# The first weight tile on ACT's own DMA queue, and a new order of the first ACT and DVE steps, in a two-block transformer forward pass

## What is computed

```python
def rmsnorm(x, g):
    x32 = x.astype(jnp.float32)
    y = x32 * lax.rsqrt(jnp.mean(x32 * x32, axis=-1, keepdims=True) + EPS)
    return y.astype(x.dtype) * g

def dilated_mixer(h, w_in, w_out):
    ...
    proj = h @ w_in
    ...
    return y @ w_out

def first_block(x, norm_pre, norm_post, dil_w_in, dil_w_out, ...):
    h = x
    for i in range(DEPTH):
        u = rmsnorm(h, norm_pre[i])
        ...
            y = dilated_mixer(u, dil_w_in[j], dil_w_out[j])
        ...
            y = diff_mixer(u, diff_w_in[j], ...)
        h = h + rmsnorm(y, norm_post[i])
    return h

def reference(...):
    x = first_block(...)
    return second_block(x, ...)
```

## Time and profile before

| | |
|---|---|
| median of 3 runs | 2640.03 us (2639.12 to 2641.21) |
| profiled execution | 2639.08 us |
| its span on the core | 2637.8 us |
| PE busy | 2607.4 us, 99% of the span |
| DVE, POOL, ACT busy | 1250.3, 1149.4, 1038.0 us |
| share of PE in the chain that ended last | 94% |
| DMA | 282.22 MB, mean 107 GB/s |

### The profile page before, as it was taken

One profiled execution on the slowest core, in us unless ns is written; L12 is line 12 of the kernel. 1 busy time (PEld: TensorE's weight loads), 2 busy tenths in 40 slices (PEclk: granted clock), 3 DMA queues, 4 the chain that ended last, 5 costly groups with the idle time before them and its releaser, 6 DMA issues.

```text
span 2637.8 us, 35473 instructions
## 1 busy us (share of the span) xinstructions
PE 2607.4 (99%) x13561; PEld 2120.3 (80%) x13561; DVE 1250.3 (47%) x2448; ACT 1038.0 (39%) x1939; POOL 1149.4 (44%) x890
## 2 busy tenths in 40 slices
PE   8999999999999999999999999999999999999998
PEld 6888878778778877777888888887777788888887
DVE  4535354553566365446155333365544624542426
ACT  4343434443546344453333424234445233342422
POOL 4434334435343354334464445454333346444443
PEclk9999999999999999999999999999999999999999
DMA  6434343333331333234442333333222435233331
GB/s 196 131 102 121 103 113 113 112 114 103 97 105 64 103 96 88 82 95 131 138 153 86 109 96 96 96 98 117 80 81 78 150 110 175 80 112 96 96 96 64
DMA packets 215121, 282.22 MB, mean 107 GB/s; under 512 B 22016, under 2 KB 155620, under 8 KB 214184
## 3 DMA queue, kind: packets, MB, share of 16 engines
q1 hardware_dynamic: 214952, 279.95, 34.5%
HBM read 246.28 MB, written 16.84 MB: 100 GB/s over the span
## 4 chain that ended last, share of the span: by engine, by line
PE 94%; DVE 3%; ACT 1%; POOL 1%; issue 1%; DMA 0%; ACTq 0%; DVEq 0%; POOLq 0%
PE banks L1808 37%; PE banks L1805 30%; PE banks L1801 13%; PE banks L1826 2%; PE banks L1940 1%; PE banks L1865 1%; PE banks L1922 1%; PE banks L2043 1%; PE banks L2070 1%; PE banks L1974 1%; PE banks L1908 1%; PE banks L2028 1%; PE banks L2056 1%; DVE AR L2553 1%; PE banks L1996 1%
## 5 line engine op out<-in xcount | busy, mean ns | idle before, releaser
L3179 POOL TENSOR_TENSOR WS<-WR,WS 128x512 fp32r<-128x512 f32 (+2 forms) x672 | 857.6, 1309 | 1015.8 <-ACT WS L2188 1015.8
L1808 PE MATMUL banks<-WS,UT 128*128 128x512 f32 (+1 forms) x3312 | 720.1, 370 | 3.1 <-DVE UT L2553 3.1
L1805 PE MATMUL banks<-UT,WS 128*128 128x512 f32 (+1 forms) x3024 | 707.4, 392 | 0.7 <-ACT AR L2377 0.7
L1805 PEld LDWEIGHTS banks<-UT,WS 128*128 128x128 f32 (+1 forms) x3024 | 561.9, 187 | 131.4 <-issue 14.7
L1808 PEld LDWEIGHTS banks<-WS,UT 128*128 128x128 f32 x3312 | 559.7, 188 | 113.8 <-issue 17.0
L2188 ACT ACTIVATE WS<-WR 128x1024 fp32r<-128x1024 f32 (+1 forms) x344 | 333.4, 1019 | 215.7 <-PE banks L1808 139.0
L1801 PE MATMUL banks<-UT,WS 128*128 128x512 f32 x1536 | 367.3, 394 | 0.0
L1801 PEld LDWEIGHTS banks<-UT,WS 128*128 128x128 f32 x1536 | 283.4, 188 | 64.4 <-issue 7.0
L1808 PE MATMUL banks<-WS,AT 128*128 128x512 f32 x1296 | 300.3, 390 | 0.9 <-ACT WS L2188 0.5
L1808 PEld LDWEIGHTS banks<-WS,AT 128*128 128x128 f32 x1296 | 242.4, 188 | 52.1 <-ACT WS L2188 1.3
L3177 POOL TENSOR_TENSOR WS<-WR,WS 128x512 fp32r<-128x512 f32 x128 | 182.2, 1455 | 226.4 <-ACT WS L2184 226.4
(11 more groups left out here) (225 smaller groups left out, 2534.0 us busy)
## 6 DMA issues: line engine op xcount, KB each, us to landing
WR<-in_w_in SPq DMA_DIRECT2D x112, 512.0 KB, 3.6
WR<-in_w_up SPq DMA_DIRECT2D x88, 512.0 KB, 3.5
WR<-in_dil_w_in SPq DMA_DIRECT2D x64, 512.0 KB, 3.7
WR<-in_w_down SPq DMA_DIRECT2D x40, 512.0 KB, 3.7
WR<-in_diff_w_in SPq DMA_DIRECT2D x32, 512.0 KB, 3.7
WR<-in_dil_w_in SPq DMA_DIRECT2D x32, 256.0 KB, 3.4
AR<-AF SPq DMA_DIRECT2D x128, 64.0 KB, 2.7
AR<-AF SPq DMA_DIRECT2D x64, 128.0 KB, 2.5
```

The lines of the kernel that those rows point to most:

```text
L1805: mm = pe.matmul(B[bank][0:c, :], w[part][:, kk, g * P:g * P + c], act[:, other, kk, :], start=start, stop=stop)
L1808: mm = pe.matmul(B[bank][:, off:off + n], act[:, other, before_k + kk, g * P:g * P + P], w[part][:, kk, :], start=start, stop=stop)
L3179: ge.tensor_tensor(slot(i, 1)[:, s], raw(i)[:, s], slot(i, 0)[:, s].bitcast(F32), ALU.subtract).then_inc(lo_p.sem, 1)
```

## The change

Three things are done. First, the four transfers of tile 0 are issued by ACT, ahead of everything else in ACT's program, and no longer by SP; a helper `load_on` issues them on either engine. Second, in the list of steps the split of tile 0 half 1 and the squares of x1 are put ahead of the turn of x0. Third, DVE's low part of that half is taken out of the split (`lo_apart`) and becomes a step of its own, `lo_half`, behind the norm of x1; SP's reload of the buffer half goes with it. The number of transfers and of instructions on DVE, POOL and PE stays as it was.

```diff
+    @staticmethod
+    def lo_apart(i, v):
+
+        return (i, v) == (0, 1)
+
...
         self.step("norm", "x", 0)
         self.step("split", 0, 0)
+        self.step("split", 0, 1)
+        self.step("square", "x", 1)
         self.step("turn", "x", 0)
         self.turned_to[0] = True
-        self.step("split", 0, 1)
         self.splits = 1
         self.step("norm", "x", 1)
+        self.step("lo_half", 0, 1)
         self.step("norm", "x", 2)
         self.fill(2)
...
+        def load_on(engine, i, v):
+            _, k, n, pieces = tiles[i]
+            dst = raw(i).rearrange("p (k n) -> p k n", k=k)
+            part = slice(v * k // 2, (v + 1) * k // 2)
+            for c, src in pieces:
+                engine.dma_start(dst[:, part, c:c + src.shape[2]], src[:, part, :]).then_inc(tile_in[2 * (i % 2) + v].sem, 16)
+
         def scalar():
             se = nc.scalar
+            for v in range(2):
+                load_on(se, 0, v)
...
-                elif kind == "norm":
+                elif kind == "square" or kind == "norm" and tuple(a) != ("x", 1):
...
                         for v in halves or (0, 1):
+                            if order.lo_apart(i, v):
+                                continue
                             s = slice(v * h, v * h + h)
                             ve.wait_ge(hi.sem, hi.at[i, v])
...
+                elif kind == "lo_half":
+                    i, v = a
+                    h = tiles[i][1] * tiles[i][2] // 2
+                    s = slice(v * h, v * h + h)
+                    ve.wait_ge(hi.sem, hi.at[i, v])
+                    tt(slot(i, 1)[:, s], raw(i)[:, s], slot(i, 0)[:, s].bitcast(F32),
+                       ALU.subtract).then_inc(lo_v.sem, 1)
...
             sy.dma_start(IDN, tab[:, C_ID:C_ID + 128]).then_inc(id_in, 16)
-            load_tile(0)
             for b in (1, 2):
                 sy.dma_start(x_at[:, b, :], x_by_rest[b]).then_inc(x_in[b], 16)
             load_tile(1)
...
+                elif kind == "lo_half":
+                    i, v = a
+                    sy.wait_ge(hi.sem, hi.at[i, v])
+                    sy.wait_ge(lo_v.sem, lo_v.at[i, v])
+                    load_half(i + 2, v)
```

More of the change, by code:

```diff
@@ L1268, in build @@
                     hi.plan((a[0], v))
-                    if not order.by_pool(a[0]):
+                    if not order.by_pool(a[0]) and not order.lo_apart(a[0], v):
                         lo_v.plan((a[0], v))
+            elif kind == "lo_half":
+                lo_v.plan(tuple(a))
             elif kind == "lo":
@@ L3206, in load_half @@
             def load_half(i, v):
[L3207 to L3211, removed]
+                load_on(sy, i, v)
             def load_tile(i):
```

## The result

| | before | after |
|---|---|---|
| median, 16 runs each | 2639.72 us (2638.17 to 2641.33) | 2646.11 us (2643.52 to 2646.53) |
| profiled execution | 2639.08 us | 2644.21 us |
| its span | 2637.8 us | 2642.9 us |

The ratio is 1.0021, with a 95% interval of 1.0014 to 1.0028. The changed kernel is slower, by an amount at the very bound of 0.2%. The median lies 6.4 us higher, the profiled execution only 5.1. That difference of 1.3 us has a cause of its own, and the experiments come to it.

A forecast was written before the change was run, and what follows sets the result against it. The prediction took DVE's chain behind x0's low parts, ending at 12.13 us, as the bound. Those end 5.4 later, less 0.3 for DVE's new order: 5.1, forecast as +5.0 on 2640.03, 2645.0 us; range 2640.8 to 2647.0.

The forecast's parts named there:

- What sets the end: DVE's chain at the start: each us that the end of x0's low parts (12.13) moves also moves M2a and kernel end.
- ACT's issues: Start of ACT: four transfers taking 2.21 us plus table load leave one us before x0 lands; costed at nothing.
- one of the signs of being wrong: Squares of x0 on ACT starting later than 5.3 would mean ACT's issues or the shared start are not covered.
- T0: PE's first group, begun at 8.83 before: may be 1 us late without anyone waiting, some 4 us in the forecast.
- The landing of half 1: Tile 0 half 1 on ACT's queue: lands at 12.8 to 13.7 us, taken as 13.3.
- the rule of turns: DMA engines alternate between the two queues packet by packet, so tile 0's 1 KB packets fall behind x's 4 KB runs.
- From the high part to the low parts of x0: ACT then DVE: from the start of half 1's high part to the end of x0's low parts, 4.1 us.
- The new order on DVE: DVE behind x0's low parts: norm of x2 starts 3.9 later rather than 4.2, saving 0.3 us.
- The weights did not come in early: Rival at the start: tile 0 served early, x1 landing last; +1.2 to +2.1 us, chance 0.34.
- M1a to M2a ran at full pace: Opposite of a rival: PE's early pace reaching past M2a, +3.7 us on top, +8.7 in all, chance 0.05.
- leftovers only: Rival at the start: tile 0 gets only what SP's queue leaves, half 1 near 17 us; +8.6 us, chance 0.10.
- slower by over 0.2%: Whole kernel: more than 5.3 us slower, from the two slow cases and a tenth of the first; chance 0.24.

The follow-up runs named there:

- queue_only: Against the kernel before: tile 0's transfers issued by ACT, ACT and DVE keeping their old order of steps; 2643.43 us, ratio 1.0014.
- long_runs_128: Changed kernel with each half of tile 0 fetched in one 128-partition transfer in 4 KB runs, from other weight rows; 2641.86 us, ratio 1.0005 to the kernel before.

## Why the prediction was right, step by step

- **What sets the end.** The end of the low parts of x0 moved from 12.13 to 16.50 + 1.29 = 17.79, by 5.66; M2a by 5.33; the span by 5.1. The chain through DVE held, row by row.
- **ACT's issues.** Four issues took 2.37 us (2.21 on SP), and the table was loaded from 3.13 to 4.41. So ACT was ready 0.8 us before x0 landed by the earlier trace rows, and the cover of one us held for the issues. The squares of x0 began at 5.74, later than 5.3, so one of the signs of being wrong that the prediction had named came true: x0 landed later. Nothing waited for it in the end. It can't be read from one execution what the shared start costs there, since the squares began between 4.78 and 5.39 in the traces with tile 0 on SP's queue, and between 4.84 and 5.74 in those with it on ACT's in runs of 1 KB.
- **T0.** It began 0.8 us later, at 9.65, as DVE waited 1.14 us for the gain, and nobody waited for it: 4.3 us lay between T0's end and the first copy.
- **The landing of half 1.** The bound from below was 12.8 and the one from above 13.7; I took 13.3; it landed at 2.26 + 11.54 = 13.80. The term that was sized wrong is the 0.4 us that I credited for gaps filled by the second queue. The 0.9 us behind it was my guess at what is possible, and not worked out from a row. The packets that the changed kernel had moved by 12.6 us, to be laid beside the last line of the earlier trace rows with its 3.60 MB, and their queues:

```profile
DMA packets 2129, 3.53 MB, mean 280 GB/s; under 512 B 151, under 2 KB 1617, under 8 KB 2129
q1 hardware_dynamic: 1065, 2.50, 61.2%
q10 hardware_dynamic: 1064, 1.03, 24.3%
```

  A second queue moved no more bytes; it only changed whose bytes came first. For the mechanism the rule of turns holds, with one run at a turn: 240 of 244 successions change the queue. The Trainium skill, page "DMA: Bandwidth & Descriptors", section "Queues, rings and completion order", gives 9 to 17 descriptors as typical for what an engine takes from one queue before it changes. The trace does not agree, if a run of 1 KB or 4 KB is one descriptor, as the prediction took it. My step from that number to "tile 0 comes in early" was wrong as well: I set 9 to 17 KB of tile 0 against single runs of x. With 9 to 17 runs at a turn on both queues the bytes would still go one to four, so neither the landing of half 1 nor the equal counts could tell the two sizes apart. Only the order of the packets does.
- **From the high part to the low parts of x0.** I took 4.1 us, and it took 3.90 (13.89 to 17.79), as the first copy followed the squares of x1 by 1.04 where I had taken 1.23. This made good 0.2 of the 0.5 us by which half 1 landed later than I took. That M2a came within 0.3 us of the sum of 5.1 is luck to that extent.
- **The new order on DVE.** The norm of x2 began 5.31 us later, against 5.66 for the low parts of x0: 0.35 was saved, 0.3 was forecast. The norms of x2 and x3 stayed at 2.32 and 2.29 beside POOL, as said.
- **The rivals.** The weights did not come in early, ACT's queue was not left with leftovers, and M1a to M2a ran at full pace in both profiles of the changed kernel. M2a came 5.33 us later than before in the first profile and 5.53 in the second, where it began at 29.05. Two sums for the rivals were off: the terms of "leftovers only" make about +8.8 to +9, not +8.6, and the parts named for "slower by over 0.2%" (0.10, 0.05 and a tenth of 0.47) make 0.20, not 0.24. Neither moves the forecast of 2645.0.
- **The median.** 2646.11 lies 1.1 above the 2645.0 forecast, inside the range. It is 6.4 above before, where 5.0 was forecast. Ten of the 16 executions of the changed kernel were at 2646.0 or above, six at 2644.5 or below; of before, four of 16 were above 2641.0. What I had missed is that a fall of PE's clock in mid-kernel belongs to some executions and not to others. I had looked for the clock only at the start. The prediction has no term for it, and the median is in the range for the range's width. With the late gap filled the difference is 5.18, within 0.2 of the +5.0. The chance of 0.24 for "slower by over 0.2%" was for another cause; the point estimate of the ratio is on that bound and its interval does not settle the side.

## What to carry to other kernels

Work out which transfers must have landed before the first engine can go on, and count what stands between each of them and the queue's head in packets, not in issue time, with one packet of the other queue for each of its own: a second queue gave this kernel no bandwidth at all, and it gave the stream with the small runs the smaller share. Before a step is moved ahead on an engine that works in order, list what it waits for, since all steps behind it inherit that wait; here two copies that waited for nothing but PE inherited two transfers. And where a few us matter, look for groups in the times of the single executions and compare the profile of one of each, for a median can sit in different groups of two kernels.

## What the runs showed of the hardware that was not expected

- **Two queues on one set of DMA engines.** They took turns by single runs: 240 of 244 successions changed the queue from 9 to 10.5 us, 248 of 253 in queue_only. That made 130 packets each, 0.47 MB against 0.13 MB; a transfer of 256 KB issued at 2.26 us landed 11.54 us later, though the queue it was on held only 1.05 MB.
- **A transfer into 64 partitions.** With 4 KB runs on ACT's queue, the mean rate of both queues was 240 GB/s from 7.5 to 10 us, against 414 in the changed kernel. Whether the 64 partitions of a transfer did this was not separated from the number of transfers. It was not the source rows alone, since long_runs_128 read the same rows and had 369 in the same stretch, with packets of 4 KB at 159 ns again.
- **The clock of TensorE.** A gap of 2.45 us near 580 us, with PE busy half of 5 us, was followed in one profiled execution of the changed kernel by 3.4 us at the 1.2 GHz level, and in the other not. With 18 transposes in the gap none of 22 executions of the two kernels was above 2640.2 and 2644.9. 36 transposes laid into the gap ahead of M0a alone were followed by such a fall near 26 us, behind the next gap. What decides whether it falls was not found; that the gap is its occasion is shown by filling it.
